# Row sums of the modulation blocks: two of eight products on ScalarE, sums by 32-column matmuls inside both feed-forward stages

## The reference

```python
cs = jax.nn.silu(c)                                  # 1024 values
for layer in range(DEPTH):                           # DEPTH = 2
    mod = cs @ mod_w[layer] + mod_b[layer]           # (1024) @ (1024, 6144)
    sh1, sc1, g1, sh2, sc2, g2 = jnp.split(mod, 6, axis=-1)
    h = modulate(rms_norm(x, norm_g[layer, 0]), sh1, sc1)
    ...                                              # mixer of the layer, added to x with gate g1
    h = modulate(rms_norm(x, norm_g[layer, 1]), sh2, sc2)
    x = x + g2[:, None, :] * conv_ffn(h, ...)        # feed-forward with a short convolution
```

## Time and profile before

| | us |
|---|---|
| median of 3 executions | 1572.47 (1569.87 to 1573.28) |
| the profiled execution | 1573.68 |
| its span | 1571.9 |
| TensorE busy | 1463.6 (93%), 9806 matmuls |
| weight loads busy | 1244.4 (79%) |
| VectorE busy | 1207.0 (77%) |
| ScalarE busy | 756.6 (48%) |
| GpSimd busy | 51.5 (3%) |
| DMA | 314.72 MB, mean 200 GB/s |

### The profile page before, as it was taken

The page is one execution under the profiler, slowest core; times in us unless marked ns, Lnnn a source line. Parts: engine busy times, 40 slices in busy tenths (PEclk is TensorE's granted clock), DMA queues, the critical chain, the costliest instruction groups (busy, mean ns, idle before and its releaser), DMA issues.

```text
span 1571.9 us, 26257 instructions
## 1 busy us (share of the span) xinstructions
PE 1463.6 (93%) x9806; PEld 1244.4 (79%) x9820; DVE 1207.0 (77%) x1895; ACT 756.6 (48%) x1080; POOL 51.5 (3%) x38
## 2 busy tenths in 40 slices
PE   5598989999999899999989889999999999999998
PEld 2484468999978666999979765689998787799997
DVE  7998747999989947799995557576667768776666
ACT  3322356444454525544436567565555632365544
POOL 2501100000000000000000100000000000000000
PEclk7798999999999989999998999999999999999999
DMA  9333836878846554988853510335455433354551
GB/s 363 136 109 127 328 148 248 341 295 316 335 162 270 214 196 179 391 331 317 336 194 124 162 40 1 116 141 212 169 182 199 164 118 134 115 175 172 183 197 69
DMA packets 57320, 314.72 MB, mean 200 GB/s; under 512 B 6902, under 2 KB 8159, under 8 KB 33119
## 3 DMA queue, kind: packets, MB, share of 16 engines
q1 hardware_dynamic: 53272, 302.40, 51.2%
q10 hardware_dynamic: 3974, 11.33, 2.2%
HBM read 310.98 MB, written 1.15 MB: 199 GB/s over the span
## 4 chain that ended last, share of the span: by engine, by line
PE 71%; DVE 14%; ACT 6%; issue 5%; DMA 3%; ACTq 0%; DVEq 0%; POOL 0%; SPq 0%
PE bank L2090 58%; DVE w_lo L1213 2%; PE bank L2335 2%; ACT w_hi L691 2%; DMA raw<-in_stream 1%; PE bank L2349 1%; PE bank L2370 1%; PE bank L1976 1%; DVE hf L1426 1%; DVE arena L1251 1%; PE bank L1994 1%; ACT arena L1007 1%; DVE x L1432 1%; ACT hf L1130 1%; PE bank L2158 1%
## 5 line engine op out<-in xcount | busy, mean ns | idle before, releaser
L2090 PE MATMUL bank<-h_hi,w_hi 128*128 128x256 f32 x1928 | 554.7, 288 | 17.2 <-DVE h_lo L1414 15.6
L2090 PE MATMUL bank<-h_lo,w_hi 128*128 128x256 f32 x1928 | 547.7, 284 | 0.0
L2090 PE MATMUL bank<-h_hi,w_lo 128*128 128x256 f32 x1928 | 547.6, 284 | 0.0
L1213 DVE TENSOR_TENSOR w_lo<-raw,w_hi 128x2048 fp32r<-128x2048 f32 x186 | 426.2, 2292 | 135.7 <-ACT w_hi L691 134.5
L691 ACT ACTIVATE w_hi<-raw 128x2048 fp32r<-128x2048 f32 x186 | 355.9, 1915 | 133.0 <-PE bank L2090 74.9
L2090 PEld LDWEIGHTS bank<-h_hi,w_hi 128*128 128x128 f32 x1928 | 372.0, 193 | 19.0 <-DVE h_lo L1414 9.6
L2090 PEld LDWEIGHTS bank<-h_lo,w_hi 128*128 128x128 f32 x1928 | 372.2, 193 | 2.1 <-issue 0.7
L2090 PEld LDWEIGHTS bank<-h_hi,w_lo 128*128 128x128 f32 x1928 | 372.1, 193 | 0.0
L1629 DVE SCALAR_TENSOR_TENSOR arena<-bank,par,arena 128x255 f32<-128x255 f32 (+1 forms) x264 | 109.1, 476 | 109.9 <-ACT arena L921 77.5
L2090 PE MATMUL bank<-w_hi,a_hi 128*128 128x512 f32 x368 | 145.9, 396 | 7.1 <-DVE a_lo L1654 6.2
L2090 PE MATMUL bank<-w_hi,a_lo 128*128 128x512 f32 x368 | 145.0, 394 | 0.0
(11 more groups left out here) (299 smaller groups left out, 1774.9 us busy)
## 6 DMA issues: line engine op xcount, KB each, us to landing
raw<-in_stream SPq DMA_DIRECT2D x186, 1024.0 KB, 4.9
arena<-in_mod_stream SPq DMA_DIRECT2D x64, 768.0 KB, 6.3
arena<-in_mod_later SPq DMA_DIRECT2D x48, 512.0 KB, 5.7
raw<-in_mod_pe SPq DMA_DIRECT2D x36, 512.0 KB, 6.2
arena<-in_mod_pe SPq DMA_DIRECT2D x12, 512.0 KB, 12.2
sq<-row_store ACTq DMA_DIRECT2D x7, 512.0 KB, 3.7
sq<-in_bias SPq DMA_DIRECT2D x8, 256.0 KB, 6.6
x<-in_x_t ACTq DMA_DIRECT2D x1, 1024.0 KB, 8.8
```

The costliest lines, as they stand in the source:

```text
L1213: nc.vector.tensor_tensor(w_lo[s][:], raw[s][:], w_hi[s][:].bitcast(F32), ALU.subtract).then_inc(lo_done, 1)
L2090: ins = nc.tensor.matmul(out_, l, r, start=first and n == 0, stop=last and n == 2, **kw)
```

## The change

ScalarE makes the first two of the eight products of each block (`mod_begin`: a copy with a scale per partition, 384 columns each, into the two accumulators). VectorE waits for them and does the six multiply-adds; the addition of the two accumulators falls away. TensorE sums both accumulators: `mod_sum` does six matmuls, one for each accumulator and each third of the block, with the 32 columns `pick[:, 31-b:63-b]` (zeros, with ones in the column of the block) as the stationary operand and 128 columns of the accumulator as the moving one. They add up in bank 6, rows 32g to 32g+15 for third g, so that after 16 blocks the bank holds 96 x 128: the modulation values as rows. `open_mod` opens the bank with a matmul on zeros.

Both ffn0 and ffn1 do this inside their steps: in a turn `up_gate(2i+1)`, sum of block 3i, `down(2i)`, sum of block 3i+1, `up_gate(2i+2)`, sum of block 3i+2, `down(2i+1)`; block 15 before the last `down`. For that TensorE's loop in these two stages is written out as ten steps of straight code, and each block stands one place earlier for ScalarE and VectorE: block 0 before the loop, blocks 3i+1, 3i+2 and 3i+3 in turn i, none behind it. `mod_keep` and the sums in the latent stage are gone.

Behind the steps VectorE adds the bias to the 96 rows (`rows_out`) ahead of the four `x_add`, TensorE turns them into columns after the last `down` (`columns_turn`), and VectorE copies the columns (`columns_out`) after the four `x_add`; `mod_out` is gone. `rows_turn` 1 and 3 are gone; `store_rows` sends the rows in three DMAs of 16 x 128, with no copy on ScalarE. A new input `mod_pick` (pick and bias rows) is loaded by ScalarE's queue after the first `store_rows`, its second bias in the next stage. The instructions of GpSimd and SyncE are the same.

```diff
             def store_rows(i):
+                if i % 2:
+                    act.wait_ge(sem("gates_known"), 3 + 2 * (i // 2))
+                    for g in range(3):
+                        act.dma_start(row_store[i, 0:n * P].rearrange("(b g p) -> g b p", g=3, p=P)[g], mod_rows[32 * g:32 * g + MOD_BLOCKS, :])\
+                            .then_inc(sem("row_stored"), 16)
+                    return
...
+                def mod_begin(b, i=None):
+                    act.wait_ge(landed, n + 16 * per)
+                    if b >= len(mod_acc):
+                        act.wait_ge(sem("mod_turned"), b - len(mod_acc) + 1 + 3 * per)
+                    for e in range(2):
+                        ins = nc.scalar.activation(mod_acc[b % len(mod_acc)][:, e, :], buf[:, e, :], ACT.Copy, scale=silu_c[:, c0 + e:c0 + e + 1])
+                    ins.then_inc(sem("mod_begun"), 1)
...
-                for kt in range(DT):
+                for kt in range(2, DT):
+                    if kt == 2:
+                        dve.wait_ge(sem("mod_begun"), b + 1 + 3 * per)
...
-                    if kt < 2:
-                        ins = nc.vector.tensor_scalar(parts[e], w, c, None, ALU.mult)
...
-                nc.vector.tensor_tensor(parts[0], parts[0], parts[1], ALU.add).then_inc(sem("mod_used"), 1)
...
+            def rows_out(r):
+                nc.vector.tensor_tensor(mod_rows[:], bank[6][0:96, 0:P], row_bias[0:96, :], ALU.add).then_inc(sem("gates_known"), 1)
+            def columns_out(r):
+                nc.vector.tensor_copy(mod[:, l, 0:48].rearrange("p (b g) -> p g b", g=3),
+                                      bank[7][:, 0:96].rearrange("p (g b) -> p g b", g=3)[:, :, 0:MOD_BLOCKS]).then_inc(sem("gates_known"), 1)
...
+                if b0 is not None:
+                    mod_block(b0, c0)
...
-                    run(2 * i + 1, q0 + 2, q0 + 5, i, {0: 0, 2: 1})
-                    run(2 * i + 2, q0 + 5, q0 + 8, i, {0: 2})
+                    run(2 * i + 1, q0 + 2, q0 + 5, i, {0: 1, 2: 2})
+                    run(2 * i + 2, q0 + 5, q0 + 8, i, {0: 3})
...
-                    mod_block(b0 + 15, c0)
+                    rows_out(f)
...
+            def mod_sum(b, r):
+                pe.wait_ge(sem("mod_used"), MOD_SLOTS + 2 * (MOD_BLOCKS * r + b) + 2)
+                for e in range(2):
+                    for g in range(3):
+                        ins = nc.tensor.matmul(bank[6][32 * g:32 * g + 32, 0:P], pick[:, 31 - b:63 - b],
+                                               mod_acc[(MOD_BLOCKS * r + b) % len(mod_acc)][:, e, g * P:(g + 1) * P],
+                                               start=False, stop=b == MOD_BLOCKS - 1, skip_group_check=True)
                 ins.then_inc(sem("mod_turned"), 1)
...
+                        up_gate(s, q)
+                        mod_sum(3 * i + 2 * e, f)
+                        down(s - 1, q + 2)
+                        if not e:
+                            mod_sum(3 * i + 1, f)
...
-            ffn(1)
-            mod_turn(MB[4], range(0, 3))
+            ffn(1, MB[4])
...
-                    mod_turn(MB[4], range(3, 6))
-            mod_turn(MB[4], range(6, 11))
...
-                    mod_turn(MB[4], range(11, 14))
-            mod_turn(MB[4], range(14, 16))
```

More of the change, by code:

```diff
@@ L945, in slot_hi, with run @@
                     return a_hi[:, k:k + 2, :]
-                def run(s, q, nq, i=None):
+                def run(s, q, nq, i=None, blocks={}):
                     g = step(s, q, i)
@@ L952, in run @@
                             hi(nq + k, i)
+                        if b0 is not None and k in blocks:
+                            mod_begin(b0 + blocks[k], i)
                 g = step(0, q0)
@@ L1023, in _ @@
             store_rows(2)
-            ffn(1)
+            ffn(1, MB[4], 8)
             norm_x(BOTH)
```

127 lines of the change are left out of this document (64 added, 63 removed).

## The result

The changed kernel takes 1577.93 us (median of 20 executions) against 1572.31 for the kernel before; the ratio is 1.0040, with a 95% interval of 1.0029 to 1.0050. It is 4.6 to 7.9 us slower. A second series of the same program gave 1.0039 (1.0023 to 1.0056). The forecast of no change was wrong; the time lies just inside the stated range, near the 1577 us of rival (a), but not for (a)'s main reason.

A forecast was written before the change was run, and what follows sets the result against it. TensorE was taken to bound ffn0 and ffn1, waiting for VectorE only at their ends. Terms -3.85 - 0.2 + 6.85 - 3.6 = -0.8 us gave 1572.9 profiled, 1571.7 us median; range 1566 to 1578.

The forecast's parts named there:

- rival (a): Heads of ffn0 and ffn1: a half-clock loss in each, and 0.70 us a sum; +4.7 us, 1577 us; chance 0.18.
- VectorE is worth nothing inside the loops: Loops of ffn0 and ffn1: products and addition leaving VectorE gain nothing, as TensorE hardly ever pauses there.
- A block's sum, 0.62 to 0.64 us: TensorE, both stages: six matmuls a block cost 0.62 to 0.64 us, against 0.67 for ffn0's three one-column matmuls.
- Head of ffn0: Start of ffn0: TensorE waits for block 1 until 278.1 instead of 277.18; the next chunk starts 0.85 us later.
- Tail of ffn0, -3.85 us: End of ffn0: no wait for the last a_lo, x turned at 451.2 instead of 455.05; ffn0 in all -3.85 us.
- Head of ffn1, +3.9: Start of ffn1: TensorE waits 1.7 us for block 0 and 1.0 for block 1; with two sums +3.9 us.
- ffn1 to the turning of x, +6.85: Whole of ffn1: head +3.9, 14 more sums +8.7, a_lo in time; x turned 6.85 us later.
- Latent stage, -3.6: Latent stage: row sums of 13 blocks leave; first 5.4 us worth 1.9, next 2.0 gained in full; taken as -3.6 us.
- (d): Faster: block 1 in time in both heads, half clock after 852 spared, a sum 0.55 us; -6.5 us, 1566 us; chance 0.22.
- (b): TensorE's sums: a set of 128 columns costs what one of 256 does; +13 us, 1584 us; chance 0.07.
- (c): TensorE's loops as straight code: instruction fetches stall 0.5 us a step; +10 us; chance 0.04.
- The weighing: TensorE's sums: the skill's load rule, an estimated 0.3 us more a block, some 9 us in all, was set aside.

The follow-up runs named there:

- half the sums: The changed kernel with three matmuls for each block, not six, the sums of the odd tiles left out: 1572.54 us, 0.9999.
- the addition back: The changed kernel with the addition of the two accumulators back on VectorE and three matmuls for a block: 1575.60 us, 1.0024.
- loops written out: The kernel before with only TensorE's loops of ffn0 and ffn1 written out as ten steps: 1575.04 us, 1.0018; second series 1573.36 us, 1.0009.
- mixed: The changed kernel's way in ffn0 alone, addition on VectorE, three matmuls a block, paired sums; ffn1 as before but for ScalarE's products: 1571.09 us, 0.9982.
- waits filled: Matmuls on zeros in three TensorE waits: on the kernel before with ScalarE's two products, 0.9942 and 0.9953; on the mixed kernel, 0.9946.
- the pairs: The changed kernel with the sum of block 3i moved behind the down projection, next to that of block 3i+1: 1575.85 us, 1.0025.
- the places undone: The changed kernel with the blocks where they stood before, block 0 in the loop and block 15 behind it: 1581.38 us, 1.0063.

## Why the prediction was wrong, step by step

The forecast was -0.8 us; the three stages that the change touches gave +5.1 and +4.8. The first step that failed is the price of a block's sum, 0.62 to 0.64 us where 0.763 was measured: by the turns some 3.8 us in the two stages. The second is the latent stage's -3.6 us, a gain that was there halfway through the stage and gone at its end (-1.4 and -1.1). The third is block 15's sum ahead of ffn0's last down projection, left out of the path (0.66 us).

- **VectorE is worth nothing inside the loops.** Right: turns of 35.98 and 33.96 us with and without the two products. With the sums left as they were it is worth 2.7 us in all, 1.9 of them at ffn1's end by the rows, which the forecast counted only in part (the a_lo wait, but not the 0.6 us of block 15).
- **A block's sum, 0.62 to 0.64 us.** Mis-sized: 0.763 by the turns. The sets were right (0.109 forecast, 0.105 measured), and the loads stay hidden. Leaving was read up to the next matmul's start only, and the 0.10 us that the second matmul comes late was missed. For 15 blocks of ffn0 that is +1.3 us where -0.5 was written, for ffn1's 14 blocks 10.7 where 8.7 was.
- **Head of ffn0.** The second wait was sized right (0.85 us in both executions, forecast 1.0). The first execution had another 1.33 us ahead of it, which goes with late chunks and was not in the forecast.
- **Tail of ffn0, -3.85 us.** The step that failed is "TensorE arrives at 440.5 + 0.85 - 0.5 = 440.9". The sum of block 15 now stands ahead of the last down projection, and was not added there: 0.66 us by its rows. With the 1.8 us of the mis-sized sums and 0.4 of the head the projection started at 445.38 - 1.62 = 443.8, not 441.0 (1.62 us is what the trace was late before ffn0). From there the tail went as forecast: 10.4 us to the turning of x, 10.2 in the forecast, no wait and no half clock. In all -0.9 and -2.0 us for -3.85.
- **Head of ffn1, +3.9.** Forecast 2.7 us of waiting, found 1.43 and, in the second trace, 1.46: block 0 was ready at 650.15 - 1.01 = 649.1 and not 649.8 (1.01 us is what this trace was late there). With two sums +3.0.
- **ffn1 to the turning of x, +6.85.** Found +7.8 in both traces (+7.4 and +8.0 for the whole stage). Loop and head together were 1 us too low (+10.0 for +9.0 at the last down projection), the wait before the transposes right (4.41 us for 4.6), with half clock as forecast.
- **Latent stage, -3.6.** The step is "the last 1.3 lie where TensorE waits anyway", taken as free. The terms before it were right: the first 5.4 us of sums gave 1.7 (1.9 forecast; the 3.46 us wait for a_lo took the rest), the next gave 2.1 (2.0). At the wait ahead of the keys' turn, where the last sums had stood, the first trace is 3.5 us ahead, as forecast. That wait grew from 1.40 to 2.80 us, and 3.4 us at half clock followed it in both traces of the changed kernel; some 0.5 us more went by longer waits for ScalarE. In all -1.4 and -1.1. The place of the half clock is chance, though. In the traces with half the sums and with the addition back, no half clock follows the same 2.80 us wait, and they end at -1.44 and -1.27 all the same, since 6.8 us and not 3.4 then follow the 4.38 us wait ahead of the query heads' turn. The traces side by side, from the first big matmul behind ffn1 to the one at 922.22 in the kernel before:

| latent stage | us at half clock | traces | length of the stretch, us |
|---|---|---|---|
| as before | 3.4 | 4 | 89.28 to 89.45 |
| as before | 6.8 | 1, the kernel before | 90.72 |
| as before | 10.2 | 1, loops written out | 92.18 |
| as before | 13.7 | 1, mixed | 93.89 |
| as before, waits filled | 0, 3.4, 6.8 | 1 each | 87.87, 89.27, 90.87 |
| sums gone | 10.2 | 7, the changed kernel's two among them | 89.10 to 89.62 |

At equal half clock the sums are worth 2.6 to 3.1 us (92.18 against 89.10 to 89.62). But all seven traces without them have 10.2 us of it, and four of the seven with them and no filling have 3.4, and then there is no difference left. That taking the sums out brings the half clock on is what these traces suggest; no run changes the clock alone.

- **The rivals.** (a) had the right size (+4.7) mostly by luck: there is no stretch at half clock in either head, from which it took 3.4 us, and its 0.70 us for a sum, right in direction, is still too low. It was given 0.18. (b) and (c) fell on measurement. (d) needed heads without a wait for block 1 (0.85 and 0.63 us were found) and a sum of 0.55 us.
- **The weighing.** The Trainium skill's rule (TensorE: Matmul & The Clock Gate, The mechanism) that loads overlap only across row groups would have put an estimated 0.3 us more on a block. The blocks did cost 0.13 us more than forecast, but the half sums and the pairs put this on entering and leaving. A set of three takes 0.105 us for 128 columns, half of the 0.218 for 256, which leaves no room for a load that would cost the same in both: here, too, the rule is not seen, with all matmuls on the same rows and three column groups.

## What to carry to other kernels

Work that moves from an engine with room to the one that sets the time has to be priced by whole turns, since the cost of an interruption shows up to two instructions behind it. Small pieces are best put side by side: each interruption less was worth 0.34 us here. Before matmuls are taken out of a place, look at what TensorE does next: where it then waits longer, the clock can take the gain back. Matmuls on zeros in such waits may help. With the 4.39 us wait among those filled the medians fell by 0.25 to 0.37%; with it left open they did not fall, and the half clock stood there instead. An engine that is idle in the middle of a stage can still be late at its ends, and relief there was what paid in this change. And a stage's gain read from one trace is compared at equal half clock, or it may be the clock's.

## What the runs showed of the hardware

- Leaving 32-column f32 matmuls costs the second matmul behind them 0.10 to 0.11 us (0.34 us after the first, not 0.23). The one-column sums of the kernel before do it too: 0.59 us up to the next matmul, 0.67 by the turn.
- The same wait in the same code is followed by half clock in some executions and not in others. Behind the 2.15 us ahead of ffn1's last down projection it came in three traces and not in two; behind the 2.80 us ahead of the keys' turn in four (the changed kernel's two, the pairs, the places undone) and not in two (half the sums, the addition back). In the latent stage each 3.4 us of it cost 1.4 to 1.7 us (the table above).
- Half clock also came with no wait: for 13.6 us from the midst of 36 one-column matmuls back to back, with TensorE busy by every record, and for 3.4 us from 851.7 in the kernel before, behind the 3.58 us of such matmuls in the earlier trace rows.
- Half clock costs nothing where another engine sets the length: 14.96 us from a_lo to the turning of x, with the down projection at 0.73 us or at 0.47 us for its first matmul.
